# Seven-product sets in a new order: lower left product sixth, upper left block accumulated by TensorE onto ScalarE's copy

## What is computed

```
x = x + 0.5 * swiglu_ffn(rmsnorm(x, ffn1_norm), ffn1_w_gate, ffn1_w_up, ffn1_w_down)
x = x + hybrid_mixer(rmsnorm(x, mix_norm), ...)
x = x + 0.5 * swiglu_ffn(rmsnorm(x, ffn2_norm), ffn2_w_gate, ffn2_w_up, ffn2_w_down)
swiglu_ffn: (silu(x @ w_gate) * (x @ w_up)) @ w_down      # hidden width 2816
```

## Time and profile before

| | |
|---|---|
| median of 3 runs | 1777.34 us (1776.34 to 1778.88) |
| profiled execution | 1777.71 us, span 1775.90 us |
| TensorE busy | 97% of the span |
| VectorE, ScalarE, GpSimd busy | 57%, 40%, 4% |
| granted TensorE clock, mean | 0.995 |
| seven-product sets, first FFN | from 938.55 to 1205 us |
| seven-product sets, second FFN | from 1466.9 to 1733 us |

### The profile page before, as it was taken

How to read it: one execution, slowest core, us unless ns; L and a number is a source line. 1 busy time by engine, 2 the same in 40 slices (tenths; PEclk the granted TensorE clock), 3 DMA queues, 4 the chain that set the end, 5 groups by cost and what they waited for, 6 DMA issues and landing times.

```text
span 1775.9 us, 21351 instructions
## 1 busy us (share of the span) xinstructions
PE 1721.1 (97%) x8703; PEld 1277.9 (72%) x8703; DVE 1010.5 (57%) x1489; ACT 704.5 (40%) x1144; POOL 78.9 (4%) x78
## 2 busy tenths in 40 slices
PE   7999999998999999999999999999999999999998
PEld 6878888885454545454477788898877887788896
DVE  4768865643333333333457866765577457856765
ACT  4556435441111111111335445454355435545453
POOL 0000000000000000000001111100000001111100
PEclk9999999998999999999999999999999999999999
DMA  6222225547999999999947888883303167898781
GB/s 216 94 72 72 95 81 180 193 154 289 421 421 420 421 421 421 420 421 421 372 122 170 213 201 196 179 190 124 119 0 107 49 194 185 192 220 196 166 200 56
DMA packets 117512, 385.74 MB, mean 217 GB/s; under 512 B 7088, under 2 KB 22592, under 8 KB 91424
## 3 DMA queue, kind: packets, MB, share of 16 engines
q1 hardware_dynamic: 88928, 318.33, 46.7%
q0 software_dynamic: 26176, 61.78, 18.9%
q10 hardware_dynamic: 2304, 4.20, 0.6%
HBM read 364.36 MB, written 6.29 MB: 209 GB/s over the span
## 4 chain that ended last, share of the span: by engine, by line
PE 85%; DVE 9%; ACT 5%; issue 1%; DMA 0%; SPq 0%; DVEq 0%; ACTq 0%
PE PS L1491 12%; PE PS L1600 8%; PE PS L1602 8%; PE PS L1601 8%; PE PS L1524 6%; PE PS L1630 6%; PE PS L1632 6%; PE PS L1631 6%; PE PS L1634 3%; PE PS L1636 3%; PE PS L1635 3%; DVE lo L2386 2%; PE PS L1462 2%; PE PS L1463 2%; PE PS L1534 2%; PE PS L1708 2%
## 5 line engine op out<-in xcount | busy, mean ns | idle before, releaser
L2386 DVE TENSOR_TENSOR lo<-raw,hi 128x1024 fp32r<-128x1024 f32 (+2 forms) x273 | 328.1, 1232 | 199.1 <-ACT hi L1939 195.6
L1939 ACT CAST hi<-raw 128x1024 fp32r<-128x1024 f32 (+2 forms) x275 | 282.4, 1066 | 220.9 <-PE PS L1602 142.9
L1600 PE MATMUL PS<-hi,xh_ffn 128*128 128x512 f32 (+1 forms) x320 | 118.5, 370 | 6.3 <-issue 4.0
L1602 PE MATMUL PS<-hi,xl_ffn 128*128 128x512 f32 (+1 forms) x320 | 117.6, 368 | 0.0
L1601 PE MATMUL PS<-lo,xh_ffn 128*128 128x512 f32 (+1 forms) x320 | 117.5, 367 | 0.0
L1491 PE MATMUL PS<-raw,XG 128*64 128x512 f32 x352 | 117.1, 593 | 0.0
L2346 DVE TENSOR_TENSOR HF<-SG,PS 128x512 f32<-128x512 f32 x16 | 17.4, 1090 | 164.8 <-PE PS L1491 164.8
L2361 DVE SCALAR_TENSOR_TENSOR YL<-PS,SM,YH 128x512 fp32r<-128x512 f32 x30 | 21.1, 746 | 138.8 <-ACT YH L1922 138.8
L2369 DVE TENSOR_TENSOR x_sb<-x_sb,PS 128x512 f32<-128x512 f32 x128 | 78.2, 678 | 8.7 <-PE PS L1535 8.7
L1905 ACT COPY HT<-PS 128x512 f32<-128x512 f32 x16 | 9.4, 586 | 175.1 <-PE PS L1500 175.1
L1634 PE MATMUL PS<-xTh,hi 128*128 128x512 f32 x192 | 78.3, 408 | 0.4 <-DVE lo L2386 0.3
(11 more groups left out here) (520 smaller groups left out, 4237.5 us busy)
## 6 DMA issues: line engine op xcount, KB each, us to landing
raw<-in_w_in SPq DMA_DIRECT2D x26, 1024.0 KB, 5.1
rawz<-in_w_down_experts SPq DMA_DIRECT2D x25, 1024.0 KB, 10.9
raw<-in_w_up_experts SPq DMA_DIRECT2D x24, 1024.0 KB, 16.0
raw<-in_w_gate_experts SPq DMA_DIRECT2D x20, 1024.0 KB, 15.5
raw<-in_ffn_w_down SPq DMA_DIRECT2D x20, 1024.0 KB, 6.0
rawz<-in_w_up_experts SPq DMA_DIRECT2D x19, 1024.0 KB, 19.1
raw<-in_w_down_experts SPq DMA_DIRECT2D x16, 1024.0 KB, 12.0
rawz<-in_w_gate_experts SPq DMA_DIRECT2D x16, 1024.0 KB, 13.8
```

Source lines behind the costliest of these rows:

```text
L1600: e.matmul(o, xh[:, k, c], h[:, k, :], start=k == 0 and not more, stop=False, skip_group_check=more)
L1602: x = e.matmul(o, xl[:, k, c], h[:, k, :], start=False, stop=k == 3, skip_group_check=more)
L1939: e.copy(q.hi[:, a:b], q.raw[:, a:b]).then_inc(*a_hi((u, 0) if part == 0 else u))
L2386: e.tensor_tensor(q.lo[:, a:b], q.raw[:, a:b], q.hi[:, a:b].bitcast(F32), ALU.subtract).then_inc(*v_lo(key))
```

## The change

The last two products change places: A22 x T4, the lower left one, is sixth, S4 x B22 seventh, and `BANK` and the added quarter follow. The upper left block is no longer added by VectorE: ScalarE copies bank 0 after product 1 into bank 2 (`first_onto_second`: step `R1` in a G set, `seed` in a D set), product 2 accumulates onto that, and Silu reads the bank. `R4` is replaced by `R0` (a copy of bank 4), and `C22`, `C21`, `sgb`, `hb` come earlier, `ht` and its turn later. A G product is walked in two halves of its depth (both tiles, then both again), with a semaphore at its middle; the next-but-one weight block's first half is cast and subtracted directly behind it (`split_first`), before `behind[j]`. In a D set the steps of the left operands are placed anew. Cut to its core:

```diff
     def split_to(self, j):
         while self.split < min(j, len(self.units)):
-            if self.halves and self.units[self.split].four:
+            if self.units[self.split].four:
                 u = self.first + self.split
-                self.steps.extend([("hi", u, 0), ("hi", u, 1), ("lo", u, 0), ("lo", u, 1)])
+                if self.rounded:
+                    self.steps.extend([("hi", u, 1), ("lo", u, 1)])
+                else:
+                    self.steps.extend([("hi", u, 0), ("hi", u, 1), ("lo", u, 0), ("lo", u, 1)])
                 self.split += 1
+                self.rounded = False
                 continue
...
+
+    def split_first(self):
+        u = self.first + self.split
+        if self.split < len(self.units) and self.units[self.split].four and self.units[self.split - 2].by_halves:
+            self.steps.extend([("hi", u, 0), ("lo", u, 0)])
+            self.rounded = True
...
-        self.plan = [self.t3, self.b11, self.b21, self.t2, self.t1, self.b22, self.t4]
-
-
-SEVEN = ("S3", "A11", "A12", "S2", "S1", "S4", "A22")
-BANK = (4, 0, 2, 0, 0, 0, 4)
-PAST = {3: 1, 4: 3, 5: 4, 6: 0}
-QUARTER = [(1, 1), (0, 0), (0, 0), (1, 0), (1, 1), (0, 1), (1, 0)]
+        self.plan = [self.t3, self.b11, self.b21, self.t2, self.t1, self.t4, self.b22]
+
+
+SEVEN = ("S3", "A11", "A12", "S2", "S1", "A22", "S4")
+BANK = (4, 0, 2, 0, 0, 4, 0)
+PAST = {2: 1, 3: 1, 4: 3, 5: 0, 6: 4}
+QUARTER = [(1, 1), (0, 0), (0, 0), (1, 0), (1, 1), (1, 0), (0, 1)]
...
+    def gates(w, at):
+        return [(w, pre, *at, t) for t in range(2)]
+
     past = None
-    feed.halves = True
     for what in SETS:
         behind = {j: [] for j in range(7)}
         ahead = []
         if past:
-            ahead = turns(*past, (0, 1))
-            behind[0] = [(w, pre, *past, t) for w in ("sgb", "hb") for t in range(2)]
+            ahead = turns(*past, (2, 3))
+            behind[0] = gates("ht", past) + turns(*past, (0, 1))
         if what[0] == "gu":
             p, cut = what[1:]
-            own = {1: ("R1",), 2: ("C11",), 3: ("sg", "R2"), 4: ("R4", "C22"), 5: ("ht",), 6: ("C21",)}
+            own = {1: ("R1",), 2: ("sg",), 3: ("R2", "R0"), 4: ("C22",), 5: ("C21", "sgb"), 6: ("hb",)}
             for j, ws in own.items():
-                behind[j].extend((w, pre, p, cut, t) for w in ws for t in range(2))
-            if past:
-                behind[0].extend(turns(*past, (2, 3)))
+                for w in ws:
+                    behind[j].extend(gates(w, (p, cut)))
             if (p, cut) == (0, 1):
                 behind[0].extend([("sum", pre, "x", "S1"), ("sum", pre, "x", "S2")] + split_left(pre, "x", "S2"))
                 behind[1].extend(split_left(pre, "x", "S1") + [("sum", pre, "x", "S4")])
                 behind[2].extend(split_left(pre, "x", "S4") + turns(0, 0, (0, 1)))
                 behind[3].extend(turns(0, 0, (2, 3)))
             if p < NS and cut:
-                j = 2 if p else 4
-                behind[j].extend([("sum", pre, p, "S3")] + split_left(pre, p, "S3"))
-                behind[j + 1].extend(split_left(pre, p, "A11"))
+                behind[4].extend([("sum", pre, p, "S3")] + split_left(pre, p, "S3"))
+                behind[5].extend(split_left(pre, p, "A11"))
             past = (p, cut)
         else:
             p = what[1]
-            behind[0].extend(split_left(pre, p, "A12") + turns(*past, (2, 3)))
-            behind[1].extend([("sum", pre, p, "S1"), ("sum", pre, p, "S2")] + split_left(pre, p, "S2"))
-            behind[2].extend(split_left(pre, p, "S1"))
-            behind[3].append(("sum", pre, p, "S4"))
-            behind[4].extend(split_left(pre, p, "S4"))
-            behind[5].extend(split_left(pre, p, "A22"))
-            for j, js in ((1, (1,)), (2, (0,)), (3, (3,)), (4, (4,)), (5, (5, 2)), (6, (6,))):
+            behind[0].extend([("sum", pre, p, "S1"), ("sum", pre, p, "S2")])
+            for j, ws in ((1, ("A12", "S2")), (2, ("S1",)), (3, ("A22",)), (4, ("S4",))):
+                for w in ws:
+                    behind[j].extend(split_left(pre, p, w))
+            behind[1][0:0] = [("seed", pre, p, t) for t in range(2)]
+            for j, js in ((2, (0,)), (3, (3,)), (4, (4,)), (5, (5,)), (6, (2, 6))):
                 behind[j].extend(("seven_x", pre, p, q, t) for q in js for t in range(2))
+            behind[2].append(("sum", pre, p, "S4"))
             past = None
         for j in range(7):
             u = feed.take((pre, *what))
             S.extend(ahead if j == 0 else ())
-            S.extend(("seven", (pre, *what), j, t, u) for t in range(2))
+            S.append(("seven", (pre, *what), j, u))
+            feed.split_first()
             S.extend(behind[j])
     p = len(FPARTS) - 1
     key = (pre, "d", p, 0)
     for ui in range(2):
         u = feed.take(key)
         if ui == 0:
-            S.extend(turns(*past, (0, 1)))
-        for i in range(4):
+            S.extend(turns(*past, (2, 3)))
+        for i in range(4) if ui else (2, 3, 0, 1):
             S.append(("mm", key, ui, i, u))
             if ui:
                 S.append(("ev", key, i))
-            elif i == 1:
-                S.extend([(w, pre, *past, t) for w in ("sgb", "hb") for t in range(2)] + turns(*past, (2, 3)))
+            elif i == 3:
+                S.extend(gates("ht", past) + turns(*past, (0, 1)))
...
+                if j >= len(at_hl) and U[first + j - 2].half and u.n <= U[first + j - 2].n:
+                    u.hl_first = [U[first + j - 2].half]
...
-            def seven(key, j, t, u):
+            def seven(key, j, u):
                 q = U[u]
...
-                pe.wait_ge(a_hi, u)
-                pe.wait_ge(v_lo, u)
                 more = j in PAST
...
-                    pe.wait_ge(a_ev, ({3: "R1", 4: "R2", 5: "R4"}[j], *at_set(key), t))
                 left_ready(pe, key, j)
...
-                for k in range(4):
...
-                    freed[b] = [(v_ev, ({2: "C11", 5: "ht", 6: "C21"}[j], *at_set(key), t))]
+                by_halves = key[1] == "gu"
+                for half, t in ((0, 0), (0, 1), (1, 0), (1, 1)) if by_halves else ((0, 0), (1, 0), (0, 1), (1, 1)):
+                    b = BANK[j] + t
+                    pe.wait_ge(a_hi, u if half else (u, 0))
+                    pe.wait_ge(v_lo, u if half else (u, 0))
+                    if not half:
+                        if not more:
+                            taken(b)
+                        elif PAST[j] == 1:
+                            pe.wait_ge(a_ev, ("R1", *key, t))
+                        elif key[1] == "s":
+                            pe.wait_ge(v_sum, ("x", key[0], key[2], PAST[j], t))
+                        elif j == 6:
+                            pe.wait_ge(v_ev, ("C22", *at_set(key), t))
+                        else:
+                            pe.wait_ge(a_ev, ({4: "R2", 5: "R0"}[j], *at_set(key), t))
+                    c = slice(t * 128, t * 128 + 128)
+                    o = PS[:, b, 0:q.n]
+                    for k in (2 * half, 2 * half + 1):
+                        e.matmul(o, xh[:, k, c], h[:, k, :], start=k == 0 and not more, stop=False, skip_group_check=more)
+                        e.matmul(o, xh[:, k, c], l[:, k, :], start=False, stop=False, skip_group_check=more)
+                        x = e.matmul(o, xl[:, k, c], h[:, k, :], start=False, stop=k == 3, skip_group_check=more)
+                    if half:
+                        x.then_inc(*p_mm((key, j, t)))
+                    elif t and by_halves:
+                        x.then_inc(*p_mm((key, j, "half")))
+                for t in range(2):
+                    b = BANK[j] + t
+                    if key[1] == "s":
+                        freed[b] = [(v_sum, ("x", key[0], key[2], j, t))]
+                    elif j == 2:
+                        freed[b] = [(a_ev, ("sg", *at_set(key), t))]
+                    elif j in (5, 6):
+                        freed[b] = [(v_ev, ({5: "C21", 6: "ht"}[j], *at_set(key), t))]
...
-                for s, k in q.hl_free:
+                for s, k in q.hl_first if part == 0 and q.hl_first else q.hl_free:
...
+            def first_onto_second(key, t, w):
+                act.wait_ge(p_mm, (key, 1, t))
+                e.copy(PS[:, 2 + t, 0:w], PS[:, t, 0:w]).then_inc(*a_ev(("R1", *key, t)))
+
...
             def R1(n, p, cut, t):
+                before_ = SETS[SETS.index(("gu", p, cut)) - 1]
+                if (p, cut) == (0, 1):
+                    act.wait_ge(v_ev, ((n, "u", 0, 0), 2 + t))
+                elif before_[0] == "s":
+                    act.wait_ge(v_sum, ("x", n, before_[1], 2, t))
+                else:
+                    act.wait_ge(a_ev, ("sg", n, *before_[1:], t))
+                first_onto_second((n, "gu", p, cut), t, FPARTS[p][cut][1] - FPARTS[p][cut][0])
+
+            def seed(n, p, t):
+                act.wait_ge(a_ev, ("sg", n, p, 1, t))
+                first_onto_second((n, "s", p), t, 512)
 
...
```

(37 more changed lines are left out.)

39 lines of the change are left out of this document (4 added, 35 removed).

## The result

The changed kernel takes 1806.3 us (1805.69 to 1808.27, 4 runs) where the kernel before takes 1776.84 (4 runs): ratio 1.0166, interval 1.0148 to 1.0183, 29.5 us more. The forecast was 1797.5 in a range of 1783 to 1812. The profiled execution took 1805.69 us for a span of 1803.9, against 1775.9 before: 28.0 more to account for.

The account below looks back on a forecast made before the run. TensorE, busy 97% of the span, was taken to bound the kernel. New waits of 40.7 us less 20.5 taken away gave net +20.2, so 1797.5 us was forecast, in a range of 1783 to 1812.

Parts of the forecast that it names:

- A: Product 2 of four down sets waits for A12, rounded behind two seed copies in ScalarE's queue: 4 x 3.3 = 13.2 us.
- B: Product 4 of four down sets waits for product 3's x_sb add in VectorE's queue: 4 x 0.2 = 0.8 us.
- C: Bottom half's turn before a down set, after G01 and G11, waits for hb: four times, 13.8 us in all.
- D: Bottom half's turn after G10 and G20, hb behind a half block's rest: 4 x 0.8 = 3.2 us.
- E: Top half's turn behind product 0 of G11 and G21, ht behind a half block: four times, 3.1 us in all.
- F: Product 2 of G01 waits for copy R1 behind XS2's cast and two weight halves: 1.75 and 0.45, sum 2.2 us.
- G: G21 to the last down projection: hb behind a whole block's cast and rest, 2 x 2.2 = 4.4 us.
- one sign of being wrong, on the clock: The prediction would be wrong in the clock if a set's stretch fell under 1.00.
- the clock falls in the new long waits: Rival: TensorE's clock drops after waits over 3 us; 13 us more at four places (1811), 26 at eight (1824); chance 0.11.
- Taken away: Writing a weight block's first half 2.7 us earlier and starting on it removes 14 waits and two small ones: 20.5 us.
- The copy from bank to bank: ScalarE's seed copy, priced at 0.54 us like copies from bank to SBUF; uncertainty -2 to +2 us on the sum.
- VectorE keeps up: Rival: only the waits before products 2 and 4 of the down sets stay; net -6.5, 1771 us; chance 0.09.

Follow-up runs that it names:

- experiment 6: Changed kernel with seeds, S3/A11, gate products and x_sb addition requeued, plus R1 ahead of the half block and of XS2's rounding in G01: 1758.61 us, ratio 0.9895.
- Experiments 7: Kernel before with only products by halves and the early cast of the first half, old order, no seed copies: 1777.97 us, ratio 1.0003.
- 8: Changed kernel without the early cast; TensorE still starts a product on the first rounded half: 1797.74 us, ratio 1.0114.
- 10: Kernel before with only TensorE's start on the first rounded half of a block, blocks still cast whole, old order: 1772.96 us, ratio 0.9974.
- 11: Changed kernel with all queue edits, without the early cast and without the start on the first half, so products wait for whole blocks: 1769.01 us, ratio 0.9949.
- experiment 9: Changed kernel with all queue edits and without the early cast, TensorE's start on the first half kept: 1759.19 us, ratio 0.9892.

## Why the prediction was right, and where it was off

**Right: the direction, the places and nearly all sizes of the new waits.** Measured as what a product or turn took beyond one that waits for nothing:

| term | forecast | measured |
|---|---|---|
| A, product 2 of the down sets | 13.2 | 4 x 3.07 = 12.3 |
| B, product 4 of the down sets | 0.8 | 0 |
| C, turn before the down sets | 13.8 | 4 x 3.12 = 12.5 |
| D, turn after G10 and G20 | 3.2 | 4 x 0.72 = 2.9 |
| E, turn behind product 0 of G11 and G21 | 3.1 | 4 x 0.72 = 2.9 |
| F, product 2 of G01 | 2.2 | 1.84 + 0.54 = 2.4 |
| G, before the last down projection | 4.4 | 2 x 2.0 = 4.0 |
| sum | 40.7 | 37.0 |

With 20.5 taken away that is 16.5 net, 3.7 under the 20.2 of the forecast. The long walks came out 0.2 to 0.4 too long, a few hundredths per step: for A in D0 the steps were 0.20, seed 0.48, 1.08 to the rest, 1.14 and 0.14, in sum 3.04 instead of 3.23. At F the profile names the rest of the second weight half, not the copy; the two ended within 0.04 us (948.90 and 948.86). By the code the product's start waits for the first half, long done, and the copy, so the forecast's reason stands; experiment 6, which moved the copy, agrees.

The signs listed came too: four waits of 2.9, four of 2.7, two of 1.6 (2.0 with what stands around them) and eight of 0.35. So did one sign of being wrong, on the clock: stretches at 0.96 and 0.93.

**Off: the step "the clock falls in the new long waits" stood as a rival with 0.11, and it is what happened.** Six stretches, 10.6 us, more than a third of the loss. The forecast had taken the clock as 1.00; its rows told that 1.75 us of waiting left it alone and 5.43 did not, and a case between the two deserved more than 0.11. The trace of the kernel before held a nearer case that the forecast passed over: in the first block TensorE resumed at 384.21 from a wait of only 1.23 us, and 2.6 us later the clock was low:
```profile
383.00:386.70 3.70, 2.49 (x23) 2.52 (x24) 3.43 (x6) 2.75 (x4) 0.00 (x0) 1.00 0.00 0
386.80:390.10 3.30, 3.30 (x11) 2.62 (x10) 2.41 (x5) 3.02 (x5) 0.00 (x0) 0.50 0.02 5
```
The rival's price was off too: 3.25 each, from 6.5 us at half clock, where five of the six stretches here lasted a little over 3 us and cost 1.5 to 1.6, and one of 6 us cost 2.7. With that, and with new waits 3.7 us smaller than forecast, the result lies between the forecast and the rival's 1811. The forecast's own spread, 1790 to 1805, doesn't reach it: that the stated range does is owed to this rival, and the two errors, 3.7 too much wait and 10.6 of clock left out, partly cancel, which is luck. The rule in the Trainium skill, TensorE: Matmul & The Clock Gate, section HAM oscillation, that a long enough gap puts the clock back, was thus the one to follow: by that rule, the trace agrees at 2.9 us in all 16 profiled cases of the table below, and at 2.7 us in 5 of 10.

**Right total, wrong reason: the paragraph "Taken away".** It gave the 20.5 us to the weight block that may be written half a product earlier. Experiments 7, 8 and 10 show that this early cast gives nothing: it costs 5.0 us on the old order (1777.97 against 1772.96) and 8.6 in the changed kernel, as its rests stand ahead of the gate products (D, E, part of C) and of R1 (F). What took the old waits away is the other half of that sentence, TensorE's start on the first half, together with the new order: experiments 10 and 11 price the start at 4.4 us on the old order and 9.8 on the new one with its queues repaired. That the sum of 20.5 came out is luck in so far as its reason failed.

**B was sized under cover of A.** The 2.9 us wait before product 2 let VectorE catch up. With A gone, B is 4 x 1.9.

**The copy from bank to bank.** Taken as 0.54; it took its queue 0.48, and 0.57 from start to end. The changed kernel's copies (least, median and most, in ns), and the kernel before's copies from a bank into SBUF (RA):
```profile
L2037 ACT COPY PS<-PS x28: 463/570/577, 948.4 to 1739.1; 128x512 f32<-128x512 f32 x20, 128x384 f32<-128x384 f32 x8
```
```profile
L2024 ACT COPY RA<-PS x20: 479/587/589, 965.9 to 1725.0; 128x512 f32<-128x512 f32 x12, 128x384 f32<-128x384 f32 x8
```
0.570 against 0.587 us: the rule in the Trainium skill, ScalarE: Activation LUTs, section Step-by-step: what each stage is for, that writing PSUM is faster than writing SBUF, has the sign right, with 0.017 us at this size. Copies into two SBUF tiles of the kernel before differ by 0.010 among themselves (0.577 into RB, 0.587 into RA), so the difference is small against what else moves it, and nothing hangs on it.

**VectorE keeps up (0.09)** did not happen, but the edits bring it about: experiment 9 has the changed kernel's arithmetic and is 1.1% faster than the kernel before. The forecast's reason against that rival, that average room does not shorten a chain, held as far as the queues stood as written.

**Open.** Why the clock falls at some waits of about 2.7 or 1.8 us and not at others like them, and how often it does over many executions.

## What to carry to other kernels

When an edit frees a resource earlier, look at what the freed work now stands in front of: the early cast cost 5.0 us on the old order and 8.6 on the new one, because its rest was queued ahead of a product that TensorE needed next, and nothing once the queues were repaired. Put what an engine's next instruction waits for first in each queue, and repair all waits of a stretch together, since one long wait hides the next in line. Price waits of the length seen here, 1.8 to 2.9 us on TensorE, with a chance of 1.5 us of low clock behind each: it came at 4 of 12 from 1.8 to 2.3 us, 5 of 10 at 2.7 and 16 of 16 at 2.9.
